# A two-layer hybrid encoder on one core: x passed in both layouts, head scaling one phase sooner, spatial matrices passed transposed

## The chip, the core and the metric

The kernel runs on one core of a Trainium2 chip. The time is device microseconds of one launch, as a median of several runs. The core's engines are TensorE (PE, with its weight loads as PEld), VectorE (DVE), ScalarE (ACT), GpSimd (POOL) and SyncE (SP), which here only issues DMAs. Each runs its own instruction stream in order; they wait for one another by semaphores.

## The reference, cut to what matters

```python
for l in range(2):                                   # x: (512, 1024) float32
    h = rmsnorm(x, norm_g[l])
    proj = h @ w_in[l]                               # all branches and gates
    qa, ka = rope(a_q, positions), rope(a_k, positions)
    out_a = sliding_window_attention(qa, ka, va, sinks[l]) * silu(a_gate)
    # spatial gating: 8 groups, a masked 128x128 mixing matrix for each
    w = where(mask, sp_w[l], 0)
    sv = einsum('gts,bnsgc->bntgc', w, layernorm(gelu(b_v))) + sp_b[l]
    out_b = gelu(b_u) * sv * silu(b_gate)
    # gated linear recurrence, 4 heads, then a norm for each head and token
    oc = rmsnorm(hgrn2_chunkwise(c_q, 1 - f, c_i, log(f)), hgrn_norm_g[l])
    out_c = oc * silu(c_gate)
    y = sum(sigmoid(merge + b_merge[l]) * (branches @ w_branch[l])) @ w_out[l]
    x = x + y
return rmsnorm(x, final_g)
```

## The kernel before

**Layout.** Features lie on the partitions, tokens (512) on the free axis. Every projection is a product of a weight tile 128x128 with an h tile 128x512. To keep float32 accuracy each operand is split into a high part (rounded to fp32r) and a low part (the difference), and each product is three: high x high, high x low, low x high (`three`, lines 536 to 538). The norm's gain is folded into h; the factor of each token, rstd, is applied when results leave PSUM (the tile RS, `rstd`).

**Units and jobs.** The weights come in units of 256 columns (1 MB each, 512 KB for `mix`). A unit has two jobs; job n belongs to unit n // 2. Jobs 0 and 1 (unit 0, keys and values) run interleaved over the eight k tiles (`project_both`); all others one after the other (`project`, 24 products of 512 columns for a full job). Units 1 and 2 (jobs 2 to 5) are the queries, units 3 to 8 belong to the recurrence, 9 and 10 (jobs 18 to 21) to the spatial branch, 19 onward (job 38 onward) to merge gates and mixing. Job n needs both low halves of its unit; `claim` waits for them.

**Splitting.** For unit v ACT writes both high halves (`split_hi`, line 861), POOL the low part of the first half (`split_lo`, line 1206), DVE that of the second (`split_lo`, line 1317). Unit 0 is different: two quarters and a half, all by DVE.

**Order of each engine.** Written out by hand: each engine walks through phases 0, 1, 2, ..., one for each job. In phase n DVE and ACT do what is listed for `phase[n]` and then the evacuation of job n (`evac`), which waits for job n on PE; PE runs `hooks[n]` right after job n. In an even phase ACT and POOL split unit n // 2 + 1 first; DVE does its half first up to phase 6 and from phase 36 on, else in the middle of the phase. A waiting instruction holds everything behind it on its engine.

**The opening.** SP loads the constants, x by quarters of its columns (512 KB each, tokens on partitions) between the pieces of unit 0, then unit 1, the positions, unit 2. PE transposes x tile by tile into PSUM (line 490; `transpose_x(k)`), ACT makes the high part of h from PSUM (line 876), DVE the low part (line 1305), ACT copies x itself to SBUF (line 880, `x_evac`). Tiles 2 to 7 are transposed between the products of jobs 0 and 1. Between these DVE takes the row statistics of x (bn_stats, line 1334). Then come `first_rstd` on ACT (a square root, ahead of job 0's evacuation), `rstd_diagonal` on DVE (line 1385), and after job 2 on PE four sums with a matrix of ones (line 823), which ACT copies to RS (`rstd_row`, phase 2, line 1099). DVE then does `angle_rest` (lines 1297 to 1300), ACT the sines (line 1090), DVE `trig` and five rotations (`rope`, lines 1460 to 1463; phases 3, 3, 4, 4, 5). The first attention scores (after job 7) wait for all five rotations.

**Heads.** The recurrence works on two pairs of heads. For pair p, PE writes the output (`recurrent_out`, after job 36 for p = 1), ACT takes squares and a root (`head_squares`, line 1050), DVE scales (`head_scaled`, line 1660), PE transposes (`transpose_heads`, line 722), DVE takes the result (`heads_taken`). For p = 1 `head_scaled` is in phase 38 and the transposes after job 38; for p = 0 in phase 25 and after job 25.

**Spatial matrices.** `side(layer)` loads them with rows on partitions; PE transposes the eight after job 19 (line 729), ACT copies them out (line 1056), DVE zeroes the masked block.

The products of one k tile, the order of DVE's opening, and the place of head scaling:

```python
pe.matmul(bank, wh, ah, start=first, stop=False)
pe.matmul(bank, wh, al, start=False, stop=False)
return pe.matmul(bank, wl, ah, start=False, stop=final)
...
phase[at_["khat"] + 4].append((head_scaled, p))
phase[at_["khat"] + 5].append((heads_taken, p))
```

Of the kernel before, what the change touches and what calls it, by code (L numbers as in the profile page):

```python
# [24 lines left out]
P = 128  # L25
KT = D // P
TB = T // P
# [29 lines left out]
for _k in KIND:  # L57
# [9 lines left out]
              last_taken=19, carry_exp=19, decayed=20, khat=21),  # L67
         dict(block_diffs4=24, block_exp4=25, block_ops=26, first_exps=27, first_ops=28, first=28, second_exps=29,
              first_taken=29, second_ops=30, last_exp=31, last_ops=31, second=31, second_taken=32, last=32,
              last_taken=33, carry_exp=33, decayed=34, khat=34))  # L70
# [35 lines left out]
def build(nc, x, positions, w_in, b_merge, w_branch, w_out, norm_g, final_g, attn_sinks, sp_w, sp_b,  # L106
# [9 lines left out]
    with ctx:  # L116
# [23 lines left out]
        SPW = at("sp_w_rows", [P, 8, P], r_ob)  # L140
# [100 lines left out]
        def sem(name):  # L241
# [4 lines left out]
            side_in=16 * 6, pj_done=NJ, act_evac=sum(e == "a" for e, _ in EVAC_NO),  # L246
# [5 lines left out]
            state_ready=2, oc_done=2, oc_root=2, oc_scaled=2, ocT_done=2, oc_ready=2, wT_done=1, wT_evac=1, wT_ready=1,  # L252
# [35 lines left out]
        wT_done, wT_evac, wT_ready = lsem("wT_done"), lsem("wT_evac"), lsem("wT_ready")  # L288
# [11 lines left out]
        fill_done, xT_done, xT_evac = sem("fill_done"), sem("xT_done"), sem("xT_evac")  # L300
# [118 lines left out]
        def x_bank(k):  # L419

            return (M[2:] + PJ)[k % 6]

# [4 lines left out]
        def _(sp):  # L427
# [3 lines left out]

            buf, src = unit_load(0)
            sp.dma_start(CST[:, :], consts[:, :]).then_inc(cst_in, 16)
            load_x(0)
            sp.dma_start(buf[:, 0:2, :], src[:, 0:2, :]).then_inc(first_in[0], 16)
            load_x(1)
            sp.dma_start(buf[:, 2:4, :], src[:, 2:4, :]).then_inc(first_in[1], 16)
            load_x(2)
            sp.dma_start(buf[:, 4:8, :], src[:, 4:8, :]).then_inc(raw_in[0], 16)
            load_x(3)  # L440
            load_weights(sp, 1)
            sp.dma_start(POSI[:, :], positions[0].partition_broadcast(P)).then_inc(pos_in, 16)
            load_weights(sp, 2)

            def side(layer):
                sp.dma_start(SPW[:, :, :], sp_w[layer].rearrange("g t s -> t g s")).then_inc(side_in, 16)
# [8 lines left out]
            for v in range(RB, DEPTH * NU):  # L455
# [6 lines left out]
                load_weights(sp, v)  # L462
                if v == RB + 1:
                    sp.wait_ge(p_trig, 1)
                    side(0)
# [15 lines left out]
        def _(pe):  # L481

            def transpose_x(k):
                if k % 2 == 0:
                    pe.wait_ge(x_in[k // 2], 16)
                if k >= 6:
                    pe.wait_ge(xT_evac, k - 5)
                    pe.wait_ge(xg_lo, k - 5)
                for tb in range(TB):
                    last = pe.transpose(x_bank(k)[:, tb * P:(tb + 1) * P], XTOK[:, tb, k * P:(k + 1) * P], ID)  # L490
                last.then_inc(xT_done, 1)

# [10 lines left out]
            transpose_x(0)  # L503
# [5 lines left out]
            def program(layer):  # L509
# [30 lines left out]
                def project_both(n, layer):  # L540
# [3 lines left out]
                    for k in range(KT):  # L544
                        if n == 0 and layer == 0:
                            if k in (1, 2, 3):
                                if k == 2:
                                    pe.wait_ge(p_vec, 1)
# [1325 lines left out]
```

## Time and profile before

| | us |
|---|---|
| median of 3 runs | 1010.35 (1008.8 to 1011.27) |
| the profiled execution | 1009.57 |
| its span, first to last instruction | 1007.8 |
| PE busy | 994.3 |
| DVE busy | 624.2 |
| ACT busy | 498.4 |
| POOL busy | 291.6 |

The profile is of one execution. Busy time is summed over the instructions of an engine; a wait isn't busy. PE's matmuls overlap, so products start every 0.23 us though each is given about 0.39 us. A view in order of time (a timeline) merges neighbours of one kind into one row with their count.

### The profile page before, as it was taken

The numbers are of one execution on the slowest core, as the hardware profiler recorded it, in microseconds if no ns is written. First come the engines' busy times: TensorE is split into PE (matmuls) and PEld (weight loads), VectorE is DVE, ScalarE is ACT, GpSimd is POOL, SyncE is SP. The second block draws the span as 40 slices with busy tenths as digits, with TensorE's granted clock in tenths as the row PEclk, the third lists the DMA queues.
The fourth block names the chain that finished last, engine by engine and source line by source line (L and its number), as shares of the span: only waits on it lengthen the run. The fifth ranks groups of instructions, "written<-read, shape, count | busy, mean of one in ns | idle before, by whom it ended". The sixth has DMA issues, their size and how long they took to land.

```text
span 1007.8 us, 15922 instructions
## 1 busy us (share of the span) xinstructions
PE 994.3 (99%) x6678; PEld 840.2 (83%) x6678; DVE 624.2 (62%) x864; ACT 498.4 (49%) x837; POOL 291.6 (29%) x148
## 2 busy tenths in 40 slices
PE   8999999999999999999999999999999999999997
PEld 7888998888788888888888989988887888888886
DVE  6889966797435353536638798398944535353652
ACT  6975676655523232223366866566553333333333
POOL 2222116324312232324112121162243222223330
PEclk9999999999999999999999999999999999999999
DMA  7532122222033232324243222222222323232602
GB/s 227 159 101 76 53 85 84 84 85 85 23 104 95 94 116 82 115 72 138 84 136 107 65 82 86 85 84 61 84 87 68 119 67 112 74 117 82 199 1 83
DMA packets 93431, 94.73 MB, mean 94 GB/s; under 512 B 2272, under 2 KB 91568, under 8 KB 93360
## 3 DMA queue, kind: packets, MB, share of 16 engines
q1 hardware_dynamic: 93232, 93.68, 30.2%
q8 instruction: 52, 0.85, 0.4%
q14 instruction: 19, 0.16, 0.0%
q10 hardware_dynamic: 128, 0.04, 0.0%
HBM read 91.62 MB, written 2.10 MB: 93 GB/s over the span
## 4 chain that ended last, share of the span: by engine, by line
PE 96%; ACT 2%; DVE 1%; issue 1%; POOL 0%; DVEq 0%; ACTq 0%; POOLq 0%
PE pj L536 28%; PE pj L538 27%; PE pj L537 27%; PE mx L536 2%; PE mx L538 2%; PE mx L537 2%; PE mx L636 1%; PE mx L743 1%; PE mx L613 1%; PE mx L682 1%; PE mx L710 1%; PE mx L621 1%; ACT w_hi L861 1%; DVE w_lo L1317 1%; PE mx L713 1%
## 5 line engine op out<-in xcount | busy, mean ns | idle before, releaser
L1206 POOL TENSOR_TENSOR w_lo<-w_raw,w_hi 128x1024 fp32r<-128x1024 f32 (+1 forms) x89 | 197.9, 2223 | 547.6 <-ACT w_hi L861 547.6
L536 PE MATMUL pj<-h_hi,w_hi 128*128 128x512 f32 x832 | 328.0, 394 | 0.2 <-issue 0.2
L538 PE MATMUL pj<-h_hi,w_lo 128*128 128x512 f32 x832 | 324.1, 390 | 0.0
L537 PE MATMUL pj<-h_lo,w_hi 128*128 128x512 f32 x832 | 324.0, 389 | 0.0
L861 ACT ACTIVATE w_hi<-w_raw 128x1024 fp32r<-128x1024 f32 (+1 forms) x179 | 159.0, 937 | 163.6 <-PE pj L538 163.6
L1317 DVE TENSOR_TENSOR w_lo<-w_raw,w_hi 128x1024 fp32r<-128x1024 f32 (+1 forms) x90 | 172.7, 1919 | 79.9 <-ACT w_hi L861 79.7
L536 PEld LDWEIGHTS pj<-h_hi,w_hi 128*128 128x128 f32 x832 | 156.2, 188 | 33.2 <-issue 1.7
L538 PEld LDWEIGHTS pj<-h_hi,w_lo 128*128 128x128 f32 x832 | 156.2, 188 | 33.0
L537 PEld LDWEIGHTS pj<-h_lo,w_hi 128*128 128x128 f32 x832 | 156.3, 188 | 31.2
L1427 DVE TENSOR_TENSOR merge_gate<-pj,rstd 128x512 f32<-128x512 f32 x48 | 33.2, 691 | 164.7 <-PE pj L538 164.7
L979 ACT ACTIVATE merge_gate<-merge_gate,small 128x512 f32<-128x512 f32 x48 | 34.3, 715 | 95.6 <-DVE merge_gate L1427 95.6
L536 PE MATMUL pj<-branch_hi,w_hi 128*128 128x512 f32 x192 | 75.1, 391 | 0.0
L538 PE MATMUL pj<-branch_hi,w_lo 128*128 128x512 f32 x192 | 74.8, 389 | 0.0
L537 PE MATMUL pj<-branch_lo,w_hi 128*128 128x512 f32 x192 | 74.7, 389 | 0.0
L536 PE MATMUL pj<-w_hi,h_hi 128*128 128x256 f32 x256 | 73.7, 288 | 0.0
L537 PE MATMUL pj<-w_lo,h_hi 128*128 128x256 f32 x256 | 72.4, 283 | 0.0
L538 PE MATMUL pj<-w_hi,h_lo 128*128 128x256 f32 x256 | 72.4, 283 | 0.0
L1206 POOL TENSOR_TENSOR branch_lo<-full,branch_hi 128x512 fp32r<-128x512 f32 x24 | 32.9, 1377 | 90.6 <-ACT branch_hi L1069 77.2
L536 PEld LDWEIGHTS pj<-w_hi,h_hi 128*128 128x128 f32 x256 | 49.0, 191 | 0.6
L537 PEld LDWEIGHTS pj<-w_lo,h_hi 128*128 128x128 f32 x256 | 49.1, 192 | 0.0
L538 PEld LDWEIGHTS pj<-w_hi,h_lo 128*128 128x128 f32 x256 | 49.0, 192 | 0.0
L538 PEld LDWEIGHTS pj<-branch_hi,w_lo 128*128 128x128 f32 x192 | 36.0, 188 | 7.6
(273 smaller groups left out, 1419.8 us busy)
## 6 DMA issues: line engine op xcount, KB each, us to landing
w_raw<-in_w_in SPq DMA_DIRECT2D x61, 1024.0 KB, 5.5
w_raw<-in_w_branch SPq DMA_DIRECT2D x24, 512.0 KB, 3.4
w_raw<-in_w_out SPq DMA_DIRECT2D x6, 1024.0 KB, 5.2
x_tokens<-in_x SPq DMA_DIRECT2D x4, 512.0 KB, 6.9
w_raw_last<-in_w_out SPq DMA_DIRECT2D x2, 1024.0 KB, 8.4
sp_w_rows<-in_sp_w SPq DMA_DIRECT2D x2, 512.0 KB, 6.1
out<-out_low SPq DMA_DIRECT2D x4, 256.0 KB, 2.0
out<-out_high SPq DMA_DIRECT2D x4, 256.0 KB, 2.3
```

The costliest lines, as they stand in the source:

```text
L536: pe.matmul(bank, wh, ah, start=first, stop=False)
L537: pe.matmul(bank, wh, al, start=False, stop=False)
L538: return pe.matmul(bank, wl, ah, start=False, stop=final)
L613: last = pe.matmul(M[half][rows, cols], QP[d, j, queries], keys[d, held], start=True, stop=True)
L621: last = pe.transpose(M[half][:, tb * P:(tb + 1) * P], PR[:, half, tb, :], ID)
L636: last = pe.matmul(M[2][o, q0:q0 + 64], values[:, tb, v], PT[:, half, q0:q0 + 64], start=True, stop=True)
L682: last = pe.matmul(bank[g * 32:(g + 1) * 32, hb * 16:(hb + 1) * 16], blk, upper, start=True, stop=True)
L861: act.activation(hi_part(v, half), raw_part(v, half), ACT.Copy).then_inc(w_hi, 1)
L979: act.activation(GM[:, i % 2, t, :], GM[:, i % 2, t, :], ACT.Sigmoid, bias=bm[:, c:c + 1])\
L1206: return pool.tensor_tensor(out=dst, in0=full, in1=hi.bitcast(f32), op=ALU.subtract)
L1317: dve.tensor_tensor(out=lo_part(v, half), in0=raw_part(v, half), in1=hi_part(v, half).bitcast(f32), op=ALU.subtract).then_inc(w_lo_vec if ...
L1427: dve.tensor_tensor(out=GM[:, i % 2, t, :], in0=src, in1=RS[:, :], op=ALU.mult)\
```

## The change

- **x also comes with its axes exchanged** (`xT`, made before the launch). SP loads it in eight tiles of 256 KB straight to where `x_evac` used to put it, between the pieces of unit 0. `transpose_x`, `x_evac` and PE's waits for them go. ACT and DVE make h's parts from SBUF. x with tokens on partitions is loaded too, after unit 1 and the positions and ahead of unit 2, for the row statistics only.
- **The row statistics** (all 16 bn_stats) leave the place between the low parts: `statistics()` is the first item of DVE's phase 0, after unit 1's low part and the small bounds operations, ahead of `angle_rest`. `rstd_diagonal` goes to phase 1 (behind `angle_rest`), ACT's `first_rstd` to phase 1 (behind job 0's evacuation), PE's four sums from after job 2 to after job 3, `rstd_row` to phase 3.
- **Scores** for query tile j wait for j + 2 rotations, not for all five.
- **Heads**: for p = 1 `head_scaled` moves from phase 38 to 37, transposes stay after job 38; for p = 0 scaling stays in phase 25, transposes go from after job 25 to after job 26 and `heads_taken` from phase 26 to 27.
- **Spatial matrices** come transposed from outside (made before the launch). SP loads them, 512 KB, behind unit 11's load and a wait for the last attention product; PE's transposes and ACT's copies go.

```diff
-              last_taken=19, carry_exp=19, decayed=20, khat=21),
+              last_taken=19, carry_exp=19, decayed=20, khat=21, scaled=25, heads=26),
-              last_taken=33, carry_exp=33, decayed=34, khat=34))
+              last_taken=33, carry_exp=33, decayed=34, khat=34, scaled=37, heads=38))
...
+            def load_xT(k):
+                sp.dma_start(XT[:, k, :], xT[k * P:(k + 1) * P, :]).then_inc(xT_in[k], 16)
+
             sp.dma_start(CST[:, :], consts[:, :]).then_inc(cst_in, 16)
-            load_x(0)
+            load_xT(0)
             sp.dma_start(buf[:, 0:2, :], src[:, 0:2, :]).then_inc(first_in[0], 16)
-            load_x(1)
+            load_xT(1)
+            load_xT(2)
             sp.dma_start(buf[:, 2:4, :], src[:, 2:4, :]).then_inc(first_in[1], 16)
-            load_x(2)
+            load_xT(3)
+            load_xT(4)
             sp.dma_start(buf[:, 4:8, :], src[:, 4:8, :]).then_inc(raw_in[0], 16)
-            load_x(3)
+            for k in range(5, KT):
+                load_xT(k)
             load_weights(sp, 1)
             sp.dma_start(POSI[:, :], positions[0].partition_broadcast(P)).then_inc(pos_in, 16)
+            for j in range(KT // 2):
+                load_x(j)
             load_weights(sp, 2)
...
+                if v % NU == UNITS.index(("ag", 0)):
+                    sp.wait_ge(pv_done, counted(v // NU)(pv_done, A_HEADS // 2))
+                    sp.dma_start(WT[:, :, :], sp_w[v // NU]).then_inc(wT_in, 16)
...
                         if n == 0 and layer == 0:
-                            if k in (1, 2, 3):
-                                if k == 2:
-                                    pe.wait_ge(p_vec, 1)
-                                transpose_x(2 * k)
-                                transpose_x(2 * k + 1)
                             if k == KT // 4:
-                                pe.wait_ge(w_lo, 1)
+                                pe.wait_ge(p_vec, 1)
+                                pe.wait_ge(quarter_lo, 2)
...
+                    pe.wait_ge(rope_done, upto(rope_done, j + 2))
                     if j == 0:
-                        pe.wait_ge(rope_done, upto(rope_done, 5))
                         pe.wait_ge(k_swapped, upto(k_swapped, 1))
...
-                    if n == 2 and layer == 0:
-                        pe.wait_ge(xT_evac, KT)
-                        pe.wait_ge(fill_done, 1)
+                    if n == 3 and layer == 0:
                         pe.wait_ge(p_diag, 1)
...
             def first_h(k):
-                act.wait_ge(xT_done, k + 1)
-                act.activation(HH[:, k, :], x_bank(k)[:, :], ACT.Copy, scale=VL[:, 0, k:k + 1]).then_inc(xg_hi, 1)
+                act.wait_ge(xT_in[k], 16)
+                scaled_hi(k, 0).then_inc(xg_hi, 1)
...
                 if layer == 0:
-                    phase[0].append((first_rstd,))
-                    phase[2].append((rstd_row,))
+                    phase[1].append((first_rstd,))
                     phase[2].append((bounds_exp,))
                     phase[2].append((first_sines,))
+                    phase[3].append((rstd_row,))
...
+            def statistics():
+                for j in range(KT // 2):
+                    last = x_stats(j)
+                pchain(last)
+                for tb in range(TB):
+                    last = dve.bn_aggr(MV[:, tb, :], XS[:, tb, :, :])
+                pchain(last)
+                pchain(dve.tensor_tensor(out=MS, in0=MV[:, :, 0], in1=MV[:, :, 0], op=ALU.mult))
+                dve.tensor_tensor(out=MS, in0=MS, in1=MV[:, :, 1], op=ALU.add).then_inc(p_ms, 1)
...
                 if layer == 0:
-                    phase[0].append((rstd_diagonal,))
+                    phase[0].append((statistics,))
                     phase[0].append((angle_rest,))
+                    phase[1].append((rstd_diagonal,))
                     phase[2].append((trig,))
...
-                    phase[at_["khat"] + 4].append((head_scaled, p))
-                    phase[at_["khat"] + 5].append((heads_taken, p))
+                    phase[at_["scaled"]].append((head_scaled, p))
+                    phase[at_["heads"] + 1].append((heads_taken, p))
```

## Rows read from the trace of the kernel before

**Rows 1.** The page, first part: busy time of each engine, share and instructions.

```profile
PE 994.3 (99%) x6678; PEld 840.2 (83%) x6678; DVE 624.2 (62%) x864; ACT 498.4 (49%) x837; POOL 291.6 (29%) x148
```

**Rows 2.** Waits of PE: who waited for whom, total us, times, longest.

```profile
PE mx L722 <- DVE attnT L1660: 3.4, 2, 1.7
```

**Rows 3.** Timeline of PE, opening: start, us, engine, line, operation, tiles, count, [idle].

```profile
9.62 0.47 PE L536 MATMUL mx<-h_hi,w_hi 128*128 128x512 f32 x1 [1.85 <-DVE w_lo L1328]
...
11.09 0.60 PE L490 MATMUL mx<-consts,x_tokens 128*128 128x128 f32 x4
...
11.88 0.47 PE L536 MATMUL mx<-h_hi,w_hi 128*128 128x512 f32 x1
...
23.32 0.39 PE L536 MATMUL pj<-h_hi,w_hi 128*128 128x512 f32 x1
...
35.50 0.48 PE L536 MATMUL pj<-h_hi,w_hi 128*128 128x512 f32 x1
...
46.91 0.47 PE L536 MATMUL pj<-h_hi,w_hi 128*128 128x512 f32 x1 [0.23 <-issue]
```

**Rows 4.** Timeline of DVE, 20 to 47 us.

```profile
20.75 1.51 DVE L1317 TENSOR_TENSOR w_lo<-w_raw,w_hi 128x1024 fp32r<-128x1024 f32 x1
22.19 1.39 DVE L1334 BATCH_NORM_STATS2 x_stats<-x_tokens 128x6 f32<-128x256 f32 x4
...
24.55 0.58 DVE L1369 TENSOR_TENSOR lb_work<-lb_work 128x4 f32<-128x4 f32 x1
...
26.11 0.18 DVE L1383 RECIPROCAL small<-small 128x4 f32<-128x4 f32 x1
26.32 0.69 DVE L1385 TENSOR_TENSOR rstd_diagonal<-consts,small 128x512 f32<-128x512 f32 x1
...
29.56 2.91 DVE L1300 SCALAR_TENSOR_TENSOR turns<-angle 128x512 f32<-128x512 f32 x1
...
37.56 0.69 DVE L1460 TENSOR_TENSOR rope_cos<-q_raw,cos 128x512 f32<-128x512 f32 x1
...
45.60 1.21 DVE L1317 TENSOR_TENSOR w_lo<-w_raw,w_hi 128x1024 fp32r<-128x1024 f32 x1
```

**Rows 5.** Timeline of PE after job 19: the spatial transposes and the next product.

```profile
142.09 1.09 PE L729 MATMUL mx<-consts,sp_w_rows 128*128 128x128 f32 x8
142.94 0.36 PE L536 MATMUL pj<-w_hi,h_hi 128*128 128x256 f32 x1
```

**Rows 6.** Timelines of ACT, DVE and PE around job 38, 250 to 278 us.

```profile
260.25 0.30 ACT L1050 ACTIVATE small<-small 128x8 f32<-128x8 f32 x1
...
267.98 1.29 DVE L1660 TENSOR_TENSOR attnT<-mx,small 128x512 f32<-128x512 f32 x2
...
267.25 0.39 PE L538 MATMUL pj<-h_hi,w_lo 128*128 128x512 f32 x1
269.33 1.09 PE L722 MATMUL mx<-consts,attnT 128*128 128x128 f32 x8 [1.69 <-DVE attnT L1660]
```

**Rows 7.** Unit 1's load: its issue on SP; size, us from issue to landing.

```profile
5.96 1.75 SPq L405 DMA_DIRECT2D w_raw<-in_w_in  x1
...
w_raw<-in_w_in SPq DMA_DIRECT2D x1, 1024.0 KB, 10.8
```

**Rows 8.** Timeline of POOL, opening: low halves of units 1 and 2.

```profile
18.76 2.42 POOL L1206 TENSOR_TENSOR w_lo<-w_raw,w_hi 128x1024 fp32r<-128x1024 f32 x1 [17.77 <-ACT w_hi L861]
...
29.52 2.41 POOL L1206 TENSOR_TENSOR w_lo<-w_raw,w_hi 128x1024 fp32r<-128x1024 f32 x1 [2.80 <-ACT w_hi L861]
```

**Rows 9.** Timeline of ACT, opening: unit 1's high halves, the root, job 2's evacuation.

```profile
17.57 2.06 ACT L861 ACTIVATE w_hi<-w_raw 128x1024 fp32r<-128x1024 f32 x2
...
24.67 0.30 ACT L1085 ACTIVATE small<-small 128x4 f32<-128x4 f32 x1 [0.82 <-DVE small L1365]
...
35.12 0.59 ACT L939 ACTIVATE q_halves_swapped<-pj 32x512 f32<-32x512 f32 x1
```

**Rows 10.** Stretches at the end: us, busy and count by engine, clock, DMA, GB/s.

```profile
1001.00:1002.00 1.00, 0.76 (x4) 0.29 (x2) 0.14 (x1) 0.00 (x0) 0.00 (x0) 1.00 0.48 178
...
1004.00:1005.00 1.00, 0.00 (x0) 0.00 (x0) 0.69 (x1) 0.66 (x1) 0.00 (x0) 0.73 0.00 0
```

## What the change should do to the time

> **What bounds the kernel now.** I read the page first: TensorE (PE) is busy 994.3 us, 99% of the span [rows 1]. So the time is PE's own work plus its few waits, and an edit pays only if it takes work or a wait from PE, or fails to add one. Next the list of PE's waits: the largest are two of 1.7 us before the transposes of the recurrence heads (line 722) [rows 2], then one of 1.85 us before the first product, for a weight's low part (line 1328) [rows 3]. Last the timelines of PE, DVE, ACT and POOL in the opening, because the change reorders that stretch. What the reader is to see there: PE has no wait between 9.62 and 46 us, but DVE hardly stops either [rows 3, 4]. DVE's low part of unit 3 starts at 45.60, takes 1.21 us, and job 6 starts right behind it at 46.91, after 0.4 us of waiting. Two engines end the opening together, and work taken from one of them is worth nothing if the other becomes later.
>
> **Part 1, spatial matrices come transposed.** Eight PE transposes per layer go. From their first (142.09) to the next product (142.94) is 0.85 us on PE [rows 5]; with two layers that is **-1.7 us**. ACT's copy-out goes too, but ACT isn't late there. Instead SP loads 512 KB after the last attention product, and SP stands in that wait with unit 12's load behind it. That load is now issued at about 142.6; even with the 10.8 us that a load of 1 MB took in the crowded opening [rows 7] it is in by 153.4, and ACT may split it only when jobs 20 and 21 are over, 142.9 + 2 x 5.8 = 154.5. Price nothing; if SP came 3 us later still, every us more would delay unit 12's split, with some 7 us of cover before PE wants it. DVE's mask, in job 22's phase, reads the matrices far later still. The `side` group loses one transfer, nobody waits for it.
>
> **Part 2, the second head pair is scaled one phase sooner.** PE's last product of job 38 starts at 267.25 and would be followed after 0.23 us; the transposes start at 269.33: 1.85 us lost, in each layer [rows 2, 6]. The root they depend on is taken at 260.25 on ACT, and DVE scales only at 267.98, because unit 20's low part stands ahead of it in the phase of job 38 [rows 6]. In the phase of job 37 DVE can scale at 260.6 and be done by 262.1, 5 us before PE asks. **-3.7 us**. What is queued behind DVE's new wait: the gate product of job 35, now done at 262.8; ACT's high part of it starts about 0.4 us later than today, then unit 20's split, ready near 268.3 where PE will want it at 267.5 + 0.9 + 5.5 = 273.9. Cover of 5 us. The first pair's transposes move from job 25 to job 26 and now stand alone: one more break in the stream; a product after a break takes 0.47 instead of 0.39 us [rows 3], so +0.1 in each layer, **+0.2**.
>
> **Part 3, the opening.** What goes from PE's path: after 9.62 three times eight transposes, 11.09 to 11.88 with a slower start behind, 0.87 each, 2.6 us. The first product also starts sooner: PE's transposes of x and DVE's wait for them are gone, x in 256 KB pieces and the first weight quarter come with 592 KB instead of 848 KB ahead; I put it at 7.8, 1.8 us sooner. Were PE the bound, that is -4.4. It isn't, as the next steps show.
>
> *Unit 1.* Job 2 needs its low halves. Its load has the same 4.2 MB in the queue up to its end as before, so it lands as before at 5.96 + 10.8 = 16.8 [rows 7]. POOL starts 1.19 after ACT (18.76 - 17.57) and takes 2.42 [rows 8, 9]: 18.05 to 20.46. DVE's half, an operation with two SBUF inputs, ended 1.08 after POOL (20.75 + 1.51 against 21.18) [rows 4, 8]: 21.54. Job 2 starts at 21.6, where it started at 23.32: 1.7 ahead. PE has been done with jobs 0 and 1 since about 19.3 and has waited 2.2 us.
>
> *The row statistics.* Before, three of four groups of bn_stats lay between the low parts, free. Now all four come after DVE's 21.54, and after the three small bounds operations and a memset (24.55 to 26.11, where the reciprocal starts: 1.56) [rows 4]. From the end of the low part (22.26) to ACT's root (24.67) were 2.41 us with one group in it [rows 4, 9]; three further groups at 1.32 (four operations at 1.39, overlapping) add 3.96. Root: 21.54 + 1.56 + 3.96 + 2.41 = 29.5, against 24.67. The x rows themselves (2 MB after the positions, 340 KB/us) are in at 23.5, not late.
>
> *The diagonal.* It used to follow the root at once (done 27.01); now `angle_rest` stands before it on DVE. Three operations and the halving run 29.3 to 31.9; the fifth (line 1300) meets POOL. ACT does root, the v evacuation and unit 2's first half, so POOL starts at 31.5, ends at 33.9, and DVE ends 0.54 after it (29.56 + 2.91 against 31.93) [rows 4, 8], at 34.5. Reciprocal and diagonal take 0.9: 35.4. PE, through with job 3 at 21.6 + 2 x 5.46 = 32.5, waits 2.9 us, does the sums and the value transposes (1.25), and DVE's low part of unit 2 is ready at 36.6. Job 4 starts at 36.7, where it started at 35.50: already 1.2 us behind.
>
> *The rotations.* ACT gets the angles at 34.5 and loads its table again: sines end 36.4 (35.1 before). Then it evacuates job 2 (3.0 us, 36.4 to 39.4), and only in the phase of job 3 copies the rstd row, 40.0. Before, that copy stood ahead of job 2's evacuation, which began at 35.12 [rows 9]. The first rotation on DVE waits for it: 40.05 instead of 37.56 [rows 4], 2.5 behind. From there to unit 3's low part is DVE work without slack (8.04 us to 45.60), and POOL's half of unit 3 falls into it as before; 0 to 0.4 more for where it falls. Unit 3's low part is done at 49.4, job 6 starts at 49.5 where it started at 46.9: **+2.6 us**. The rotations 2 to 4 and unit 4's low part follow on the same engine, also full, so jobs 7 and 8 keep the 2.6. The looser wait of `scores` (j+2 rotations) gives nothing back: the rotations stand before unit 4's low part on DVE, and job 8 needs that.
>
> A rule of the Trainium skill bears on one step (SBUF — State Buffer, section "SBUF: two separate sides"): VectorE and GpSimd share a port pair as an exclusive lock, taken also by a one-input operation in a two-port mode. The trace agrees for two-input operations (2.91 against 0.69); for the one-input halving no row here shows it. By the rule the diagonal would be 0.45 later and job 6 unchanged, since ACT reaches the sines at 35.2 anyway.
>
> **Bounds of what isn't shown.** First, unit 1's landing. Rows of 2 KB instead of 1 KB could shorten the 2 MB of x, more descriptors could lengthen it; I take 0 and keep -0.7 to +0.7, which go one for one into every later step. Second, whether POOL's angle operations hold up the small bounds operations: 1.56 as seen, 0.7 if free, 2.8 if two full waits. Third, the lock on line 1300: if DVE comes first 1 to 1.7 us less. Opening from +0.6 to +4.0, taken +2.6.
>
> **Sum.** -1.7 - 3.7 + 0.2 + 2.6 = -2.6 us. On the profiled execution of 1009.57 (span 1007.8 and 1.8 around it) that is 1007.0; the median of the runs is 1010.35, 0.8 above, so 1007.8.
>
> **Rivals.**
> *PE bound in the opening (0.12).* Parts 1 and 2 as above and -4.4 in the opening: -9.6, 1000.8. For it: PE has no wait between 9.62 and 46 now [rows 3], and the change takes 2.6 us of its work. Against it: DVE's chain above has no free microsecond.
> *The chain is shorter than I have it (0.16).* The lock falls to DVE, the landing is 0.5 sooner, the bounds operations run free: opening +0.6, total -4.6, 1005.8.
> *The clock falls (0.12).* PE would be idle 2.2 us before job 2 and 2.9 before job 4. PE's last product ends at 1001.8; in the microsecond from 1004 the granted clock averages 0.73, so it was at 2.4 GHz for half of it and at 1.2 for the rest [rows 10]: it fell near 1004.5, after 2.7 us of rest; idle spells of 1.9 us [rows 3, 6] ended at the full level. How long it would stay low no row shows; at half rate for 3 to 6 us jobs 4 and 5 lose 1.5 to 3, of which 1.9 is covered by the wait for unit 3 (job 5 would end at 36.7 + 10.9 = 47.6, job 6 starts at 49.5): 0 to +1.1, a total of -1.6, 1008.8. The Trainium skill (TensorE: Matmul & The Clock Gate, section "What's actually happening") has the same two levels, the lower one for a resting array.
> *Slower: the head pair's wait comes back elsewhere (0.06).* DVE stands 5 us in its new wait with the gate product behind it, then ACT's high part, then unit 20's split and POOL's. If job 40 waits for that split as long as PE waits now, part 2 is void and the opening's loss remains: -1.7 + 0.2 + 2.6 = +1.1, 1011.5. It decides when unit 20's low part is later than 273.9; my figure is 268.3.
> *The change misses its effect in the opening and loses there more than 4 us* (x pieces slow, statistics waiting for data): up to +6, total +1, also 1011 (0.04); both with the clock on top could pass +3.
>
> **How the numbers follow.** Forecast 1007.8 with 0.50; its own range is 1006.5 to 1009. A measurement of this kernel can tell about 0.3% (3 us) from no change: faster means below 1007.3. Of the forecast case a third lies there (0.17), with the two faster rivals (0.28) less a little of the second's upper edge: 0.41. Slower by over 3 us needs two mishaps at once: 0.04. The rest, 0.55, is no difference. The range leaves out the PE-bound rival below and the slower ones above: 1004.6 to 1010.4.
>
> **What would show it.** In the changed profile: first product near 7.8; a PE wait of about 2 us before job 2, released by DVE's low part (before: none); a wait of about 3 us before the diagonal sums; job 6 at 49.5; no wait at the head transposes and none at job 40; no rows for the spatial transposes. If the first wait is missing, unit 1 landed sooner; if the second is missing, the statistics were not the late chain, and the prediction is wrong by up to 7 us.

## The result, and the profile after

The changed kernel takes 1016.50 us (median of 4 runs, 1014.59 to 1017.04), the kernel before, run beside it, 1009.58 (1008.58 to 1011.27): a ratio of 1.0056, interval 1.0044 to 1.0069. It is 6.9 us slower by the medians and 5.7 by the ratio, where 2.6 less was forecast, and lies outside the range of 1004.6 to 1010.4. The profiled execution has a span of 1014.9 us against 1007.8.

First the page's busy times, then the list of PE's waits (who waited for whom: us in total, times, longest):

```profile
PE 994.2 (98%) x6630; PEld 838.8 (83%) x6630; DVE 624.7 (62%) x864; ACT 494.2 (49%) x825; POOL 290.4 (29%) x148
```
```profile
PE mx L664 <- issue: 6.3, 2, 3.6
PE pj L530 <- issue: 2.2, 1, 2.2
PE mx L802 <- DVE rstd_diagonal L1342: 2.0, 1, 2.0
PE mx L530 <- DVE w_lo L1284: 1.9, 1, 1.9
```

PE's busy time is that of before [rows 1], although 48 of its products are gone. The waits at the head transposes [rows 2] are gone too. Two waits of the opening are new and were forecast: before the diagonal sums, and before job 6. The first line was not: 6.3 us in two pauses at line 664, the products of the recurrence's second level, which the change does not touch. "Issue" says that the view found no semaphore that ended them. It says so of the wait before job 6 as well, but there the program does wait, for the low half of unit 3: DVE finished it at 49.45 and PE started at 49.55. At line 664 it waits for nothing. Here the two pauses are on PE's timeline, one in each layer (start, us, engine, line, tiles, count, idle before):

```profile
102.70 0.38 PE L664 MATMUL mx<-level_ops 128*32 128x32 f32 x20
106.70 0.43 PE L664 MATMUL mx<-level_ops 128*32 128x32 f32 x12 [3.62 <-issue]
...
599.58 0.39 PE L664 MATMUL mx<-level_ops 128*32 128x32 f32 x22
602.69 0.28 PE L664 MATMUL mx<-level_ops 128*32 128x32 f32 x10 [2.72 <-issue]
```

PE stops inside a run of 32 like products that wait for nothing in the program. In the kernel before the same run stands unbroken:

```profile
100.08 0.46 PE L674 MATMUL mx<-level_ops 128*32 128x32 f32 x32
```

The windows around the pauses show what the first one costs beyond itself (us, busy and count by engine, granted clock, DMA share, GB/s):

```profile
106.00:107.00 1.00, 0.30 (x12) 0.30 (x12) 1.00 (x2) 1.00 (x7) 0.00 (x0) 0.58 0.00 0
107.00:108.00 1.00, 1.00 (x10) 0.83 (x3) 0.23 (x1) 1.00 (x7) 0.00 (x0) 0.50 0.09 16
...
112.00:113.00 1.00, 1.00 (x4) 0.81 (x3) 0.96 (x4) 0.99 (x1) 0.00 (x0) 0.50 0.00 0
113.00:114.00 1.00, 1.00 (x5) 0.83 (x5) 0.88 (x3) 0.98 (x2) 0.00 (x0) 1.00 0.00 0
...
602.00:603.00 1.00, 0.31 (x11) 0.27 (x10) 0.26 (x1) 1.00 (x7) 0.00 (x0) 1.00 0.02 6
```

After the pause of 3.62 us PE runs at 1.2 GHz up to 113: 6.3 us at half rate, 3.2 us lost, and that is part of why PE's busy time did not fall. After the pause of 2.72 the clock stays at its upper level. The sum of what was not forecast is 3.6 + 3.2 + 2.7 = 9.5 us in this execution, and with the -2.6 of the forecast +6.9. That is the difference of the medians and a little more than that of the ratio (5.7, interval 4.4 to 7.0), so nothing large is left over.

What ran at the time? The DMA views of the stretches 98 to 104.15 and 103.9 to 104.6 (queue, kind: packets, MB, share of 16 engines):

```profile
q1 hardware_dynamic: 1020, 1.03, 55.5%
w_raw<-in_w_in SPq DMA_DIRECT2D x1, 1024.0 KB, 7.0
...
q1 hardware_dynamic: 74, 0.06, 29.0%
q8 instruction: 1, 0.02, 9.7%
```

A 1 MB weight load, issued at 99.4, fills the queues to about 104, from 101.7 on with 300 to 400 GB/s. With its last rows, at 104.2, comes one packet of a queue called instruction; 2.5 us later PE goes on. The page counts what this queue moved in the whole span:

```profile
q8 instruction: 52, 0.85, 0.3%
```

52 packets of 16 KB are 0.85 MB. PE has 6630 products, as many weight loads and 146 others (semaphore instructions, but for two) in this trace, 13,406 instructions. Were they 64 bytes each, an assumption so far, that would be 0.86 MB, and 256 instructions to a packet. Theory A: PE's own instruction list comes in such packets; where PE reaches the end of one whose successor is held up behind a weight load, it stands still. Taking 48 products (96 instructions) off the list moved the ends of the packets to other places of the program: at the level products of layer 0 by 66 (the x transposes' 64 and two semaphore instructions), and at those of layer 1, behind the first eight spatial transposes, by 80. In each layer one came to lie in a run of the shortest products, beside a load.

The Trainium skill (Advanced Engine Details and Errata, section "ISA Cache") says that an engine's instruction cache has lines of 16 KB, 256 instructions, and only two of them. The trace agrees in the size and the count of instructions. The same section also gives TensorE 128 KB, by an estimate from its figures eight such lines. These runs look like two: each packet runs about when PE enters the one before it (table in experiment 3), and the measurement decides.

### The profile page after: what moved, and what is told of

Same layout as the page of the kernel before. It is cut to its first block, busy times and chain, and to the rows that moved or that the text cites. A ratio compares the mean times of both kernels' runs of the same rounds, so it can differ in the third digit from the quotient of the medians.

```text
span 1014.9 us, 15821 instructions
## 1 busy us (share of the span) xinstructions
PE 994.2 (98%) x6630; PEld 838.8 (83%) x6630; DVE 624.7 (62%) x864; ACT 494.2 (49%) x825; POOL 290.4 (29%) x148
## 4 chain that ended last, share of the span: by engine, by line
PE 94%; DVE 2%; DMA 2%; issue 1%; SPq 1%; ACT 0%; DVEq 0%
PE pj L530 28%; PE pj L532 27%; PE pj L531 27%; PE mx L530 1%; PE mx L532 1%; PE mx L531 1%; DMA w_raw<-in_w_in 1%; PE mx L626 1%; PE mx L726 1%; PE mx L603 1%; PE mx L672 1%; PE mx L700 1%; PE mx L611 1%; DMA w_raw<-in_w_out 1%; PE mx L703 1%
## 5 line engine op out<-in xcount | busy, mean ns | idle before, releaser
L530 PEld LDWEIGHTS pj<-h_hi,w_hi 128*128 128x128 f32 x832 | 156.9, 189 | 35.4 <-issue 3.6
```

## The experiments

Times are medians, and each ratio is against the kernel before, run beside it on the same chip. "Late load" stands for this edit. It holds one weight load in each layer, the one that stood beside the second level's products (unit 9 of the layer's list, counted from 0), until the third group of level products is done:

```
+                if v % NU == 9:
+                    sp.wait_ge(lev_done, counted(v // NU)(lev_done, 3))
                 load_weights(sp, v)
```

"Pads" are products of ones, 32x32 in fp32, into a bank that is overwritten next. Each turned out to be two products in the trace (16 + 4 + 4 of them raised the count from 6630 to 6678), so four instructions; the 48 transposes that the change took away were one product each.

**1. Sixteen pads before the diagonal's wait, four in each layer's job 19** restore the number of PE's instructions.

```
+                        pads(16, M[4])
                         pe.wait_ge(p_diag, 1)
...
+                hooks[19].append((pads, 4, M[0]))
```

> The changed kernel with 16 small products (32x32, of the matrix of ones) put on PE before its wait for the diagonal, and 4 where the spatial transposes stood, so that PE's instruction stream is again as long, at the level products of job 13, as in the kernel before. Theory A (PE's instructions are fetched in blocks; in the changed kernel one fetch falls behind a 1 MB weight load just where PE runs through many small products): the pauses of 3.6 and 2.7 us inside the level-1 products (layers 0 and 1) vanish, with them the 6.8 us at half clock; time 2.5 us below the kernel before, near 1007. Theory B (the pauses come from the new opening through DVE or ACT, or are a matter of data): the pads change nothing, time stays 5.7 to 7 us above the kernel before.

Measured: 1008.47 us (10 runs), ratio 0.9980 [0.9970, 0.9989]. Work was added and 8 us went. The run of level products at 103.81 is whole again:

```profile
103.81 0.46 PE L668 MATMUL mx<-level_ops 128*32 128x32 f32 x32
```

What is left, -2.0 against before, is near the forecast's -2.6. Ahead of the level products of layer 0 now stand two instructions fewer than in the kernel before, and in layer 1 as many (8165).

**2. The kernel before with 48 pads ahead of its first product**, in PE's idle time.

```
+            pads(48, M[0])
             pe.wait_ge(p_norm, 1)
```

> The kernel before with 48 small products (32x32) on PE in its idle time ahead of the first real product, nothing else. They shift the level products of job 13 in PE's instruction stream by 192 instructions, which together with the 64 by which the changed kernel is shorter makes one block of 256, if the blocks are that long. Theory A: a pause of 2.5 to 4 us inside the level-1 products of both layers, perhaps half clock after the longer one (3.4 us), so 5 to 10 us above the kernel before. Theory B: at most 1 us above it (the pads overlap a wait of 1.9 us).

Measured: 1017.32 us (4 runs), ratio 1.0064 [1.0049, 1.0079]. Nothing of the change is in this kernel, and it has the change's pauses (timeline of PE in both layers). Theory A says why it would: 192 instructions more are one packet of 256 less 64, and the changed kernel is 66 shorter at that place.

```profile
100.25 0.38 PE L679 MATMUL mx<-level_ops 128*32 128x32 f32 x19
103.93 0.39 PE L679 MATMUL mx<-level_ops 128*32 128x32 f32 x13 [3.31 <-issue]
...
597.98 0.33 PE L679 MATMUL mx<-level_ops 128*32 128x32 f32 x14
599.70 0.35 PE L679 MATMUL mx<-level_ops 128*32 128x32 f32 x18 [1.40 <-issue]
```

The places fit too. Two more semaphore instructions stand ahead of the first break than in the changed kernel, and it comes one product sooner, after the 19th. In layer 1 the list is 16 instructions longer than the changed kernel's, apart from the whole packet, and the break comes eight products sooner, after the 14th instead of the 22nd. A product and its weight load are two instructions. The page of this kernel counts 53 packets for 13,694 instructions:

```profile
q8 instruction: 53, 0.87, 0.4%
```

**3. The changed kernel with the late load**: PE's list is untouched, only the load moves.

> The changed kernel with one more wait on SP: unit 9's weight load (1 MB, in each layer issued just ahead of the level products of job 13) waits until the level-1 products are done. Theory A: PE's instruction block no longer queues behind that load; the pauses shrink from 3.6 and 2.7 us to under 1 us each, time 1 to 2.5 us below the kernel before. Theory A' (the pause is there at any block border, whatever DMA is under way): pauses unchanged, 6 to 7 us above. Theory B: unchanged too.

Measured: 1008.12 us (9 runs), ratio 0.9979 [0.9969, 0.9989]. The break is at the same product, but short:

```profile
102.33 0.38 PE L666 MATMUL mx<-level_ops 128*32 128x32 f32 x20
103.15 0.32 PE L666 MATMUL mx<-level_ops 128*32 128x32 f32 x12 [0.44 <-issue]
```

In the DMA view the stretch 100 to 103 now holds one packet of the instruction queue and nothing else. The packet's time in the trace, beside PE's stop and start on its timeline, gives for all breaks of this kernel, the changed one, and experiments 2 and 5 (us):

| kernel, layer | PE passes the end of the packet before | packet ran | PE stops | PE goes on | packet to start |
|---|---|---|---|---|---|
| changed, 0 | 100.7 | 104.2 | 103.1 | 106.7 | 2.5 |
| changed, 1 | 597.6 | 600.3 | 600.0 | 602.7 | 2.4 |
| 3 (late load), 0 | 100.3 | 100.5 | 102.7 | 103.2 | 2.7 |
| 3 (late load), 1 | 591.0 | 591.7 | 593.4 | 594.2 | 2.5 |
| 2 (pads in before), 0 | 98.2 | 101.6 | 100.6 | 103.9 | 2.4 |
| 2 (pads in before), 1 | 595.8 | 597.4 | 598.3 | 599.7 | 2.3 |
| 5 (128 pads), 0 | 103.4 | 106.8 | 105.8 | 109.4 | 2.6 |
| 5 (128 pads), 1 | 599.6 | 602.9 | 602.0 | 605.5 | 2.6 |

PE goes on 2.3 to 2.7 us after the packet ran, in all eight. Between the ends of two packets lie only 2.2 to 2.4 us here, because these 256 instructions are the shortest of the program. So a packet that runs 0.2 us after PE has passed the end before it leaves a break of 0.4, and one that runs 3.5 us after it, behind a load, leaves 3.6. In the kernel before two ends lie as close (97.1 and 99.6), but the packet ran at 96.5, ahead of that load's transfer, and was there in time; the next one ran at 101.4, late behind the load, and PE needed it only at 115.4. So it takes both, a late packet and a short time to the next end: elsewhere in the kernel before, the packet for the end at 721.8 ran at 718.9, 3.9 us after PE had passed the end before it, and PE did not stop.

**4. The kernel before with the heads' part alone** (the two step tables, the transposes in the gap named heads, scaling and taking in their new phases).

> The kernel before with only the head part of the change (second pair scaled in phase 37 instead of 38, first pair's transposes after job 26). PE's stream keeps its length. My step: both waits of 1.7 us at the head transposes vanish and none comes back: 3.5 us below the kernel before (1.85 in each layer less 0.1 in each). Rival (the wait comes back at the weights of job 40, since DVE holds back a gate product): no gain or up to 1 us slower.

Measured: 1007.13 us (4 runs), ratio 0.9956 [0.9940, 0.9973]: -3.4 by the medians, -4.4 by the ratio. Both waits of [rows 2] are gone from PE's list, and nothing came in their place.

**5. 128 pads before the diagonal's wait.**

```
+                        pads(128, M[4])
                         pe.wait_ge(p_diag, 1)
```

> The changed kernel with 128 small products (32x32, into a bank that is overwritten next) ahead of its wait for the diagonal of row statistics. In the first study 16 such products there and 4 in job 19 took both pauses inside the level-1 products away. Theory A (TensorE's own instructions come in packets of 16 KB, 256 instructions of 64 bytes, and it pauses when it comes to the end of one whose successor is held up behind a weight load): 128 products are 256 instructions, one whole packet, so the boundaries fall on the same products as in the changed kernel: both pauses are back, after the 20th and the 22nd level-1 product, 3 to 4 us and 1 to 3 us, and the clock falls after the first. The products take 128 x 0.033 = 4.2 us, of which 2.0 lie in the wait for the diagonal and the rest in the 2.2 us wait before job 6. Total 1014 to 1018, about 1.006 of before. Rival B (the small products help by themselves, by keeping TensorE busy or by moving the work in time by a microsecond or two): no pauses, about 1008 as with 16.

Measured: 1020.39 us (4 runs), ratio 1.0094 [1.0078, 1.0110], above the 1014 to 1018 that was expected. A step of the expectation was wrong: a pad is four instructions, so these are 512, two whole packets, and they took 8.3 us instead of 4.2. Two packets serve the test as well as one:

```profile
105.45 0.38 PE L668 MATMUL mx<-level_ops 128*32 128x32 f32 x20
109.43 0.43 PE L668 MATMUL mx<-level_ops 128*32 128x32 f32 x12 [3.60 <-issue]
...
601.60 0.39 PE L668 MATMUL mx<-level_ops 128*32 128x32 f32 x22
605.53 0.28 PE L668 MATMUL mx<-level_ops 128*32 128x32 f32 x10 [3.54 <-issue]
```

The breaks are after the 20th and the 22nd product again, though both come 2 to 3 us later. In the execution the end is 4.5 us later than the changed kernel's (span 1019.4 against 1014.9): 2.0 by which the second break starts later (the pads' 8.3 us, of which the two waits of the opening and a sooner start take the rest), 0.8 more of second pause, and 1.7 lost at half rate behind it (granted clock 0.50 from 606 to 609). The counts in the windows up to each break tell where in PE's list it is (changed kernel, this one, and experiment 2; PE's products behind the first "x", its weight loads behind the second):

```profile
0.00:104.00 104.00, 95.98 (x728) 80.94 (x728) 84.55 (x147) 70.14 (x124) 27.32 (x19) 1.00 0.49 153
0.00:601.00 601.00, 588.72 (x4020) 496.95 (x4021) 389.62 (x555) 309.41 (x522) 171.02 (x88) 0.99 0.32 101
```
```profile
0.00:107.00 107.00, 102.55 (x984) 88.06 (x984) 85.62 (x148) 70.37 (x124) 27.28 (x19) 0.98 0.47 149
0.00:603.50 603.50, 594.78 (x4276) 503.55 (x4277) 390.36 (x556) 310.19 (x524) 170.26 (x88) 0.99 0.33 101
```
```profile
0.00:102.00 102.00, 99.40 (x855) 85.14 (x855) 84.10 (x147) 73.11 (x132) 27.85 (x19) 1.00 0.46 141
0.00:599.00 599.00, 591.74 (x4148) 500.90 (x4149) 388.75 (x555) 312.80 (x530) 171.74 (x88) 1.00 0.32 99
```

Products, weight loads, and the semaphore instructions counted to the same place (17 and 88; 19 and 88 in experiment 2) make 1473 and 8129, 1985 and 8641, 1729 and 8385. Divided by 256 each leaves 193. Six breaks in three kernels stand at one place of the packet, and the seven short ones of experiments 3, 6, 7 and 12 stand there too. The page of experiment 5 has two packets more than the changed one's, for 512 instructions more:

```profile
q8 instruction: 54, 0.88, 0.4%
```

That settles theory A's count; that pads do good or harm by themselves is out.

**6. The changed kernel with the late load and the diagonal ahead of the angles** on DVE.

```
-                    phase[1].append((rstd_diagonal,))
+                    phase[0].insert(phase[0].index((statistics,)) + 1, (rstd_diagonal,))
```

> The changed kernel with the late load (1008.1 in the first study) and on VectorE the diagonal of row statistics ahead of the five angle operations instead of behind them. The diagonal would then be ready near 30, before TensorE comes to it at 32.4, so that its wait of 2.0 goes. Theory A: job 6 waits for the low half of its weights, which VectorE makes after the second rotation, and that chain runs through the sines (which start when the angles are done, 0.9 us later now); so the 2.0 are given back before job 6, whose wait grows from 2.6 to about 4.5 or 5.5: total 1008 to 1009.5, no gain. Rival D (the two waits add up, each is the path for itself): 1006, ratio to before 2 thousandths lower than with the late load alone.

Measured: 1009.48 us (11 runs), ratio 0.9991 [0.9982, 1.0000], against 0.9979 with the late load alone. PE's timeline:

```profile
32.16 1.06 PE L804 MATMUL mx<-rstd_diagonal,ones 128*128 128x128 f32 x8
...
35.83 0.47 PE L532 MATMUL pj<-h_hi,w_hi 128*128 128x512 f32 x1 [2.18 <-DVE w_lo L1275]
...
50.15 0.47 PE L532 MATMUL pj<-h_hi,w_hi 128*128 128x512 f32 x1 [1.55 <-issue]
```

The wait for the diagonal is gone, and a wait of 2.18 for unit 2's low half stands before job 4, since the angles now push that back. I had expected the wait to come back only before job 6. The wait before job 6 did not grow to 4.5 or 5.5 either; it is 1.55, because 2.18 were lost before job 4 and PE then ran at half rate for 3.4 us (granted clock 0.71 in 36 to 38, 0.50 in 38 to 40), 1.7 lost. Job 6 starts at 50.15, with the late load alone at 49.14: the end of the chain is as expected, and there is no gain. Whether there is a loss the two intervals, which overlap, don't tell. The two new waits of the opening share one chain on DVE.

**7. The opening alone** (with the looser wait of the scores), with the late load; heads and matrices as before.

> The kernel before with the opening of the change alone (x also loaded with axes exchanged, no transposes, statistics in the first jobs; heads and mixing matrices as before), and the load that falls in job 9's slot held until the third level is done, so that no pause comes from instruction fetch. Theory A (my sum, part 3): the opening costs +2.6 us net against before, from two new waits of TensorE, 2.0 before the diagonal sums and 2.2 before job 6, less the transposes' time: 1012 to 1014, ratio about 1.0025. Rival C (the opening is worth something once the pause is gone): 1010 or less, ratio at or under 1.000.

Measured: 1013.55 us (6 runs), ratio 1.0029 [1.0017, 1.0040]: +2.9 us. The opening is a loss by itself, of the size of the sum's third part. Some 0.4 of it is the short break that is left in layer 0's level products.

**8. The kernel before with heads, matrices and the late load**, its opening left alone.

> The kernel before with the opening left as it was, and the two other parts: the heads' scaling and transposes in the same job's gap as the change puts them, and the mixing matrices laid out by the host; the load in job 9's slot held until the third level is done. Theory A: the parts add: -3.7 (heads) and -1.7 (mixing matrices, TensorE's 8 transposes of each layer), 1010.5 - 5.4 = 1005.1, ratio 0.9945 to 0.996. Rival E (a pause of instruction fetch comes up at another load, since 16 instructions are gone in each layer): a new wait of over 1 us of TensorE for issue within small products, and 1006 to 1010.

Measured: 1005.08 us (5 runs), ratio 0.9938 [0.9925, 0.9950]: -5.6, forecast -5.4.

**9. The same without the late load.**

> The version with the heads' move and the mixing matrices laid out by the host (1005.1 in the study before), now without the wait that held back the load of job 9's slot. Theory A (the late load matters only where a packet boundary falls into the level products): in layer 0 nothing of TensorE's list has changed ahead of those products, so no pause comes with or without it: 1005, ratio 0.993 to 0.996. Rival G (the late load is worth something by itself): 1006.5 or more.

Measured: 1004.77 us (5 runs), ratio 0.9947 [0.9935, 0.9959]. With an unchanged list ahead of layer 0's level products there is no break, and the late load is not needed. This or 8 is the version to keep; the runs can't tell them apart.

**10. The late load alone in the kernel before**, the control.

> The kernel before with the late load alone, as the control to the runs that carry it. Theory A: the kernel before has no pause in its level products, so the late load gives and takes nothing: within 0.1 per cent of before, 1009.5 to 1011.5. Rival G: 1.5 us or more faster, ratio 0.9985 or less.

Measured: 1010.66 us (11 runs), ratio 1.0001 [0.9993, 1.0010]. It is worth nothing where no break stands beside the load, so experiments 3, 6, 7, 8 and 12 may be read as they are.

**11. The matrices' part alone**, without the late load.

> The kernel before with the mixing matrices laid out by the host and nothing else of the change: TensorE's 8 transposes and ScalarE's 2 copies in each layer are gone. Theory A: -1.7 us (8 transposes of 0.10 in each of two layers) and the boundaries of instruction packets move by 16 instructions behind job 19 of layer 0: 1008.8, ratio about 0.998, without a wait of over 1 us for issue in the small products. Rival E: such a wait in layer 1, and 1010 to 1012.

Measured: 1008.52 us (11 runs), ratio 0.9985 [0.9977, 0.9994]: -1.9 by the medians, -1.5 by the ratio. No pause in layer 1.

**12. The changed kernel with the late load and four more warm-up products.** They stand in PE's idle time ahead of the first product.

```
+            warm(4)
             pe.wait_ge(p_norm, 1)
```

> The changed kernel with the late load and four more warm-up products of ones ahead of the first product, where TensorE waits 1.9 us and was idle. In the changed kernel the first 12 products came at 0.43 us each, twice the 0.23 of the later ones. Theory A (TensorE's slow start is hidden, since VectorE's chain of statistics, rotation and low halves sets the opening): the first products come at 0.23, jobs 0 and 1 end 1 to 2 us sooner, the wait for the diagonal grows by what is won, and the total stays at that of the late load alone: 1007.5 to 1009, ratio 0.997 to 0.999. Rival F (the slow start is on the path): 1.5 to 2.5 us faster than with the late load alone, 1006 or less, ratio 0.996 or less.

Measured: 1008.29 us (12 runs), ratio 0.9980 [0.9971, 0.9989]; with the late load alone it was 0.9979. The first is the changed kernel, the second this one:

```profile
7.92 0.77 PE L530 MATMUL mx<-h_hi,w_hi 128*128 128x512 f32 x1 [1.86 <-DVE w_lo L1284]
8.49 0.63 PE L531 MATMUL mx<-h_lo,w_hi 128*128 128x512 f32 x1
...
21.78 0.39 PE L530 MATMUL pj<-h_hi,w_hi 128*128 128x512 f32 x1
```
```profile
7.56 0.47 PE L533 MATMUL mx<-h_hi,w_hi 128*128 128x512 f32 x1 [0.77 <-DVE w_lo L1287]
7.86 0.40 PE L534 MATMUL mx<-h_lo,w_hi 128*128 128x512 f32 x1
...
21.21 0.47 PE L533 MATMUL pj<-h_hi,w_hi 128*128 128x512 f32 x1 [1.75 <-DVE w_lo L1276]
34.68 1.16 PE L805 MATMUL mx<-rstd_diagonal,ones 128*128 128x128 f32 x8 [2.35 <-DVE rstd_diagonal L1345]
```

In the changed kernel PE starts at half its pace (0.43 us from product to product up to 13.6, though the windows there give a granted clock of 1.00) and is done with jobs 0 and 1 only at 21.78. Warmed up, it has 1.75 us of waiting there instead, and job 6 starts no sooner (49.40, with the late load alone 49.14). PE's slow start is covered by the chain on DVE. That the eight first transposes had kept it away is not shown: with them the products start at full pace, but in the profiles of experiments 4, 9, 10 and 11 the clock then falls too, for 3.4 us from between 9.0 and 11.1 on (experiment 4: 0.77 in 10 to 12, 0.50 in 12 to 14).

## Why the prediction was wrong, point by point

*Part 1, the matrices:* forecast -1.7, measured -1.5 to -1.9 (11). Right. SP's new wait cost nothing.

*Part 2, the heads:* forecast -3.7 and +0.2, measured -3.4 to -4.4 (4). Right. In the changed kernel DVE has scaled the second pair from 269.29 on, and PE asks at 275.97:

```profile
269.29 1.29 DVE L1617 TENSOR_TENSOR attnT<-mx,small 128x512 f32<-128x512 f32 x2
...
275.97 1.04 PE L712 MATMUL mx<-consts,attnT 128*128 128x128 f32 x8
```

That leaves the 5 us of cover that the forecast had. The rival in which the wait comes back at job 40 did not show: PE has no wait there.

*Part 3, the opening:* forecast +2.6, measured +2.9 (7), of which 0.4 is the short break. In the changed kernel job 6 starts at 49.55, forecast 49.5; the diagonal sums at 34.81, forecast 35.4, after a wait of 2.0, forecast 2.9; job 4 at 36.2, forecast 36.7. One step was wrong without harm: PE was to be done with jobs 0 and 1 at 19.3 and to wait 2.2 us. It started slowly instead, and there was no wait; warmed up, it waits 1.75 (12). I had carried the pace of before over. The prediction took a missing wait there as a sign that unit 1 had landed sooner, and that reading was wrong: unit 1's low half was ready at 21.2, near the forecast 21.5, and PE was late. Job 6 came so close partly by luck. DVE finished the angles at 33.9, not 34.5, and from there ACT took 2.6 us to the end of the sines, not 1.9: it had taken 2.6 before as well (32.47 to 35.09). The two misses nearly cancel. The rival "PE bound in the opening" is out, and so is a shorter chain.

*The lock.* The step on the fifth angle operation (line 1300 of before [rows 4]) had it meet POOL; it met the fourth, the one-input halving. DVE's timeline of the changed kernel, and of experiment 6, where POOL's operation came earlier:

```profile
28.54 2.14 DVE L1256 SCALAR_TENSOR_TENSOR angle<-turns,angle 128x512 f32<-128x512 f32 x3
30.71 2.51 DVE L1258 TENSOR_SCALAR angle<-angle 128x512 f32<-128x512 f32 x1
33.25 0.69 DVE L1259 SCALAR_TENSOR_TENSOR turns<-angle 128x512 f32<-128x512 f32 x1
```
```profile
29.03 4.34 DVE L1258 SCALAR_TENSOR_TENSOR angle<-turns,angle 128x512 f32<-128x512 f32 x3
33.40 0.43 DVE L1260 TENSOR_SCALAR angle<-angle 128x512 f32<-128x512 f32 x1
```

POOL's low half runs 30.46 to 32.92 in the first and 29.69 to 32.09 in the second. The halving takes 2.51 us against it and 0.43 without. That is what the Trainium skill (SBUF — State Buffer, section "SBUF: two separate sides") says of a one-input operation in a two-port mode; the rule, which no row of before could show, holds here. It does not hold for every one-input operation: the 16 bn_stats of the changed kernel took 0.41 us each, beside POOL's angle operations and behind them. In experiment 6 POOL met the two-input operations instead, 4.34 us for three against 2.14.

*The clock.* The rival had the clock fall in the opening, at a cost of up to 1.1 us. In the changed kernel it stayed up behind the waits of 2.0 and 2.2. In experiment 1 it did not, behind the wait of 2.2 before job 6 (windows 49 to 52 and 52 to 54):

```profile
49.00:52.00 3.00, 3.00 (x9) 2.40 (x10) 2.83 (x5) 2.93 (x6) 0.00 (x0) 0.62 0.90 313
52.00:54.00 2.00, 2.00 (x8) 1.59 (x7) 1.93 (x4) 1.99 (x4) 0.02 (x1) 0.71 0.00 0
```

Rests of 3.3 to 3.6 us in three kernels were all followed by half rate. Of the shorter ones some were and some were not: one of 2.72 was not, one of 2.18 (experiment 6) was, and one of 2.22 was in experiment 1 and was not in the changed kernel. So the length of the rest alone does not decide it. The mechanism of the rival was right; the rest that set it off in the changed kernel is one that I did not see coming.

*The step that failed* is the sum itself: it had the 48 products go from PE's path at their time alone, and every part that the change leaves alone stay as it was. Its -1.7 - 3.7 + 0.2 + 2.6 = -2.6 has no term for the place of the instructions in PE's list. The rivals held no case in which work that isn't touched gets slower, and "slower by over 3 us" had a chance of 0.04. The runs showed +9.5 us from there: two stops of 3.6 and 2.7 us in level products that the change does not touch, where a packet of PE's instructions came late behind a weight load, and 3.2 us at half rate behind the first. With the load moved, the rest of the sum is there: -2.1 by the ratio, 1.2 us of short breaks included (3). The profile of before had the sign of it, a queue of instruction packets with 52 of 16 KB beside PE's 13,500 instructions, and the prediction does not mention it. A term for it could have been estimated: 96 instructions fewer, the place of each packet's end against the runs of short products, and the loads beside them.

What stays open: what exactly sets off a packet. Counted through all 14 traces, with the ends at instruction 193 of 256 and the packets right behind a stop left aside, each packet ran between 4.7 us before and 4.4 us after PE passed the end before it. Where no load had been in the queues for 2 us it was never later than 2.2; the later ones all stand beside a load. Why a load holds a packet back was not taken apart, and no run put another of the 52 ends into short products beside another load.

## What to carry to other kernels

When PE's list is thousands of instructions long, an edit that adds or takes some shifts the ends of all later instruction packets. If a new wait "for issue" shows inside a run of short products that wait for nothing, count PE's instructions up to it, and compare with the instruction queue's packets; then shift the list by a few dummy products, or move the load, before judging the edit. And when one engine's chain sets a stretch, price a change there on that chain alone: the 2.6 us of transposes that the opening took from PE were worth nothing, and the opening, with the statistics moved from between the low parts into DVE's chain, cost 2.9. How much of that is the statistics alone no run shows.

## What the runs showed of the hardware

- PE's instructions came in packets of 16 KB, 256 instructions of 64 bytes (52 packets for 13,406 instructions, 53 for 13,694, 54 for 13,918). PE went on 2.3 to 2.7 us after a packet ran in the eight breaks of the table; in these, with a 1 MB load in the queues, the packet ran 1.6 to 3.5 us after PE had passed the end before it, and 0.2 to 0.7 without.
- 256 instructions of the shortest products took 2.2 to 2.4 us, so that even in free queues a break of 0.2 to 0.8 us was left (seven breaks in experiments 3, 6, 7 and 12).
- After a rest of 3.62 us PE ran at 1.2 GHz for 6.3 us, which cost 3.2; after one of 2.72 us it did not, after one of 2.18 in another kernel it did, for 3.4 us.
- A one-input DVE operation of 0.43 us took 2.51 beside a POOL operation; bn_stats, also of one input, took 0.41 beside POOL and alone.
- A 32x32 product in fp32 is two products in PE's list.
